# Expert columns of the last layer by one-hot products from resident rows, without a row table in DRAM

## The reference

```
s = sigmoid(t @ w_router)                       # 16 experts in 4 groups
eidx = the two best experts inside the best group
for e in range(16):
    y = (silu(t @ w_gate[e]) * (t @ w_up[e])) @ w_down[e]   # 1024 -> 512 -> 1024, float32
    out = out + combine[:, e:e+1] * y
```

## Time and profile before

| | |
|---|---|
| median of 3 runs | 1370.53 us (1370.07 to 1372.29) |
| profiled execution, its own time | 1371.52 us |
| its span, first to last instruction | 1369.4 us |
| busy: PE, PEld, DVE, ACT, POOL | 1243.1, 783.0, 622.9, 369.1, 124.5 us |
| moved by DMA | 382.73 MB, mean 279 GB/s |
| mean granted PE clock | 0.967 |

### The profile page before, as it was taken

How to read it: one execution, slowest core, us unless ns; L and a number is a source line. 1 busy time by engine, 2 the same in 40 slices (tenths; PEclk the granted TensorE clock), 3 DMA queues, 4 the chain that set the end, 5 groups by cost and what they waited for, 6 DMA issues and landing times.

```text
span 1369.4 us, 20046 instructions
## 1 busy us (share of the span) xinstructions
PE 1243.1 (91%) x8172; PEld 783.0 (57%) x8172; DVE 622.9 (45%) x1122; ACT 369.1 (27%) x599; POOL 124.5 (9%) x119
## 2 busy tenths in 40 slices
PE   4799999999999898999989957899999988998996
PEld 1577688787777633433333336787889833443443
DVE  2728467786464542211131127577876562221222
ACT  2523234442253310100100015544546420000000
POOL 0000000000022020000000020007930310000000
PEclk9999999999999999999999977999999999999998
DMA  9734469463635579999899982875354779999996
GB/s 380 292 134 198 167 246 383 132 223 123 246 123 219 215 277 343 339 355 354 307 373 401 414 315 110 334 314 213 124 154 154 309 290 367 399 387 398 398 420 250
DMA packets 59887, 382.73 MB, mean 279 GB/s; under 512 B 8912, under 2 KB 11412, under 8 KB 20308
## 3 DMA queue, kind: packets, MB, share of 16 engines
q1 hardware_dynamic: 45584, 345.00, 65.1%
q10 hardware_dynamic: 9748, 18.74, 4.2%
q0 software_dynamic: 4464, 17.71, 3.6%
HBM read 363.84 MB, written 44.84 MB: 298 GB/s over the span
## 4 chain that ended last, share of the span: by engine, by line
issue 22%; PE 19%; DMA 14%; DVE 6%; ACT 2%; POOL 2%; SPq 0%; DVEq 0%; POOLq 0%; ACTq 0%
DMA wexp<-in_expert 11%; PE bank L2045 3%; PE bank L2047 3%; PE bank L2046 3%; PE bank L2467 3%; DMA x_rows<-trow,rowid 2%; PE bank L2452 1%; PE bank L2013 1%; PE bank L2485 1%; POOL x_rows L782 1%; PE bank L2055 1%; POOL m_lo L766 1%; PE bank L2137 1%; DMA stage<-in_in 1%; PE bank L2325 1%
## 5 line engine op out<-in xcount | busy, mean ns | idle before, releaser
L2452 PE MATMUL bank<-wexp,xg 128*64 128x512 f32 (+1 forms) x1488 | 264.9, 598 | 12.4 <-DMA wexp<-in_expert 9.4
L2045 PE MATMUL bank<-h_hi,whi 128*128 128x512 f32 (+1 forms) x640 | 224.8, 351 | 15.9 <-DVE h_lo L1271 11.7
L2047 PE MATMUL bank<-h_hi,wlo 128*128 128x512 f32 (+1 forms) x640 | 219.6, 343 | 0.0
L2046 PE MATMUL bank<-h_lo,whi 128*128 128x512 f32 (+1 forms) x640 | 219.6, 343 | 0.0
L2452 PEld LDWEIGHTS bank<-wexp,xg 128*64 128x64 f32 (+1 forms) x1488 | 77.3, 125 | 164.3 <-issue 143.1
L2467 PE MATMUL bank<-wexp,act_a 128*32 128x256 f32 (+1 forms) x1072 | 150.6, 505 | 19.5 <-DMA wexp<-in_expert 15.3
L1271 DVE TENSOR_TENSOR wlo<-stage,whi 128x2048 fp32r<-128x2048 f32 x56 | 133.7, 2395 | 40.3 <-ACT whi L809 28.4
L2045 PEld LDWEIGHTS bank<-h_hi,whi 128*128 128x128 f32 x640 | 124.1, 194 | 40.0 <-issue 14.6
L1271 DVE TENSOR_TENSOR act_a<-act_s,bank 128x256 f32<-128x256 f32 (+1 forms) x47 | 17.2, 365 | 256.7 <-ACT act_s L809 256.7
L2046 PEld LDWEIGHTS bank<-h_lo,whi 128*128 128x128 f32 x640 | 123.9, 194 | 13.5 <-issue 0.5
L2047 PEld LDWEIGHTS bank<-h_hi,wlo 128*128 128x128 f32 x640 | 123.6, 193 | 13.7
(11 more groups left out here) (343 smaller groups left out, 1599.5 us busy)
## 6 DMA issues: line engine op xcount, KB each, us to landing
wexp<-in_expert SPq DMA_DIRECT2D x190, 1024.0 KB, 15.4
stage<-in_in SPq DMA_DIRECT2D x40, 1024.0 KB, 8.5
raw<-in_mod SPq DMA_DIRECT2D x18, 1024.0 KB, 7.0
stage<-in_mod SPq DMA_DIRECT2D x16, 1024.0 KB, 4.9
x_rows<-in_c_zero SPq DMA_DIRECT2D x32, 512.0 KB, 7.7
y_rows<-in_c_zero SPq DMA_DIRECT2D x20, 512.0 KB, 7.8
spare<-in_mod SPq DMA_DIRECT2D x8, 1024.0 KB, 16.9
stage<-in_out SPq DMA_DIRECT2D x8, 1024.0 KB, 4.8
```

The lines of the kernel that those rows point to most:

```text
L2045: MM(o, w[0], x_[0], start=start, stop=False)
L2046: MM(o, w[0], x_[1], start=False, stop=False)
L2047: return MM(o, w[1], x_[0], start=False, stop=stop)
L2452: ins = MM(bank[0][g * w:(g + 1) * w, :], x_[:, 2 * j + k, :], weights[:, c], start=(first_ == 0), stop=(last_ == 0))
```

## The change

In the last layer every step's columns, those of the extra items too, are made in one go by products: the stationary operand is a 128 x 128 tile of `trow`, the moving one is the step's one-hot matrix, 64 or 32 columns wide, and two products (one for each tile of tokens) add up in `bank[1]`, so that no transpose follows. That is 8 x 2 = 16 float32 products in a step. DVE makes the one-hot matrices in a ring of three (`pick_n`, `match_n`): steps 0 to 3 ahead of the loop as in the first layer, then that of step s + 4 at the end of step s, then one in each extra item, with the table row kept in `row_now`. The last layer has no `x_rows` table, no scatters, no loads to `xpick`, no `step_rows` and no `picked_out`; the 12 zeroing blocks of its table go too. `SIDE` is 4: pieces 0 to 3 of the first ranked expert have buffers of their own (the two new ones where `xpick` lay), and SP's wait for the scatters is gone. The first layer's steps are the same.

```diff
-PICKED = (4, 2)
+PICKED = 4
-SIDE = (0, 2)
+SIDE = (0, 4)
...
+        side = [at_byte(f"side{j}", [P, 2048], f32, off) for j, off in enumerate((R2 + 8 * K, GLU, R3, R3 + 8 * K))]
+        SIDE_SEMS = ("spare_a", "spare_b", "side_c", "side_d")
...
-        x_rows = [nc.dram_tensor(f"x_rows{l}", (ROWS[l], D), f32, kind="Internal").ap() for l in range(DEPTH)]
+        x_rows = nc.dram_tensor("x_rows", (ROWS, D), f32, kind="Internal").ap()
...
@@ SP @@
-                            for rows_ in (*x_rows, y_rows):
-                                if b * P < rows_.shape[0]:
-                                    load("all", "rows_zeroed", rows_[b * P:(b + 1) * P, :], A["c_zero"])
+                            for rows_ in (x_rows, y_rows):
+                                load("all", "rows_zeroed", rows_[b * P:(b + 1) * P, :], A["c_zero"])
...
-                    if l == DEPTH - 1 and (r, j) == (plan.aside, plan.side):
-
-                        sp.wait_ge(sem("all", "scattered"), sum(2 * (span(i) // P) for i in range(DEPTH)) * 16)
@@ POOL @@
-                for t in range(T // P):
+                for t in range(T // P if l == 0 else 0):
...
-                for i in range(XR - 1):
+                for i in range(XR - 1 if l == 0 else 0):
@@ ACT @@
-                for s in range(2):
+                for s in range(2 if l == 0 else 0):
                     picked_out(s)
...
-                    if s == PICKED[l] - 1:
+                    if l == 0 and s == PICKED - 1:
-                        act.wait_ge(sem("all", "scattered"), sum(2 * (span(i) // P) for i in range(l + 1)) * 16)
+                        act.wait_ge(sem("all", "scattered"), 2 * NT * 16)
...
-                    if PICKED[l] <= s <= STEPS - XR + 1:
+                    if l == 0 and PICKED <= s <= STEPS - XR + 1:
@@ DVE @@
+                def pick_step(s, first_row, w, slot):
+                    v.then(ts(adj[:, :, 0:NT], tokv[:, 4:6, 0:NT], first_row, None, SUB))
+                    m_ = match_[:, :, 0:NT * w].rearrange("p c (t w) -> p c t w", w=w)
                     at_ = iota[:, 0:w].unsqueeze(1).to_broadcast([P, NT, w])
                     for c in range(2):
                         v.step(tt(m_[:, c, :, :], at_, adj[:, c, 0:NT].unsqueeze(2).to_broadcast([P, NT, w]), ALU.is_equal))
                     v.sync()
...
+                    if l > 0 and (not isinstance(s, int) or s >= 3):
+                        dve.wait_ge(S("xT_mm"), s - 2)
+                    tt(pick_[:, slot, 0:NT * w], match_[:, 0, 0:NT * w], match_[:, 1, 0:NT * w], ADD).then_inc(S("picked"), 1)
                     dve.wait_ge(S("picked"), s + 1)
...
+                    if l == DEPTH - 1 and PICKED <= s + 4 < STEPS:
+                        pick_step(s + 4, float(plan.steps[s + 4][3]), plan.steps[s + 4][4], (s + 4) % 3)
...
                 with dve.Fori(0, count) as i:
+                    if l == DEPTH - 1:
+                        pick_step(i + STEPS, row_now[:, 1:2], E, STEPS % 3)
                     columns(i + STEPS, E)
@@ PE @@
+                def picked_columns(s, slot, w):
+                    pe.wait_ge(S("picked"), s + 1)
+                    for k in range(KT):
+                        for i in range(NT):
+                            t = row_tile(l, NT + i)[0]
+                            if isinstance(s, int) and s == 0 and k == 0:
+                                pe.wait_ge(S("h2"), NS * KT + i + 1)
+                            ins = MM(bank[1][:, k * w:(k + 1) * w], trow[:, t, k * P:(k + 1) * P], pick_n[:, slot, t * w:(t + 1) * w], start=(i == 0), stop=(i == NT - 1))
+                    ins.then_inc(S("xT_mm"), 1)
...
-                    w, r = plan.steps[s][4], s - PICKED[l]
-                    if r >= 0:
+                    w, r = plan.steps[s][4], s - PICKED
+                    if l == DEPTH - 1:
+                        picked_columns(s, s % 3, w)
+                    elif r >= 0:
...
-                for s in range(2):
+                for s in range(2 if l == 0 else 0):
                     step_rows(s)
...
-                    pe.wait_ge(S(f"xload{LAST % XR}"), row_loads(LAST) + i * 16)
-                    pe.sem_inc(sem("all", "passed"), 1)
-                    columns(LAST % XR, E)
+                    if l == 0:
+                        pe.wait_ge(S(f"xload{LAST % XR}"), row_loads(LAST) + i * 16)
+                        pe.sem_inc(sem("all", "passed"), 1)
+                        columns(LAST % XR, E)
+                    else:
+                        picked_columns(s, STEPS % 3, E)
```

More of the change, by code:

```diff
@@ L208, in hybrid_backbone @@
     E = HALF_STEP
-    ROWS = [-(-(p.extra_base + (p.extra + 1) * E) // P) * P for p in plans]
-    assert ROWS[0] == max(ROWS) and ROWS[0] // P == 20
+    ROWS = -(-(plans[0].extra_base + (plans[0].extra + 1) * E) // P) * P
+    assert ROWS // P == 20
     TWO_PI_HI, TWO_PI_LO, ROUND = 6.28125, 2 * math.pi - 6.28125, 1.5 * 2.0 ** 23
@@ L490, in hybrid_backbone @@
         row_now = at_byte("row_now", [P, 2], f32, R6 + 256)
+        pick_n = at_byte("pick_n", [P, 3, 2 * C], f32, R6 + 3 * K)
+        match_n = at_byte("match_n", [P, 2, 2 * C], f32, R6 + 4 * K + 512)
         yg = at_byte("yg", [P, 4, 2, D], f32, R1)
@@ L775, in _ @@
                 if l == 0:
-                    pool.wait_ge(sem("all", "rows_zeroed"), (sum(ROWS) // P + ROWS[0] // P) * 16)
-                pool.wait_ge(S("h2"), seqs(l) * KT + T // P)
-                pool.wait_ge(S("rowid_ok"), 1)
-                for t in range(T // P):
+                    pool.wait_ge(sem("all", "rows_zeroed"), 2 * (ROWS // P) * 16)
+                    pool.wait_ge(S("h2"), seqs(l) * KT + T // P)
+                    pool.wait_ge(S("rowid_ok"), 1)
+                for t in range(T // P if l == 0 else 0):
                     for c in range(2):
                         pool.indirect_dma_start(
-                            out=x_rows[l], out_offset=bass.IndirectOffsetOnAxis(ap=rowid[:, 2 * t + c:2 * t + c + 1], axis=0),
+                            out=x_rows, out_offset=bass.IndirectOffsetOnAxis(ap=rowid[:, 2 * t + c:2 * t + c + 1], axis=0),
                             in_=trow[:, t, :], in_offset=None,
                         ).then_inc(sem("all", "scattered"), 16)
-                pool.wait_ge(sem("all", "scattered"), sum(2 * (span(i) // P) for i in range(l + 1)) * 16)
-                for i in range(XR - 1):
-                    row, w = plans[l].steps[PICKED[l] + i][3:]
-                    load("all", f"yg{i}", xpick[0:w, i, :], x_rows[l][row:row + w, :])
+                if l == 0:
+                    pool.wait_ge(sem("all", "scattered"), 2 * (T // P) * 16)
+                for i in range(XR - 1 if l == 0 else 0):
+                    row, w = plans[l].steps[PICKED + i][3:]
+                    load("all", f"yg{i}", xpick[0:w, i, :], x_rows[row:row + w, :])
                 if l < DEPTH - 1:
@@ L1198, in _ @@
                         silu(s - 1, places[s - 1][1])
-                    if s + 2 < PICKED[l]:
+                    if l == 0 and s + 2 < PICKED:
                         picked_out(s + 2)
@@ L1767, in _ @@
                 dve.wait_ge(S("places"), 1)
+                pick_, match_ = (pick, match) if l == 0 else (pick_n, match_n)
                 if LEADERS[l]:
@@ L1773, in _ @@
                     for s in range(LEADERS[l]):
-                        v.step(tt(quick(match, s), iota[:, 0:C].unsqueeze(1).to_broadcast(shape), place[:, :, s].unsqueeze(2).to_broadcast(shape), ALU.is_equal))
+                        v.step(tt(quick(match_, s), iota[:, 0:C].unsqueeze(1).to_broadcast(shape), place[:, :, s].unsqueeze(2).to_broadcast(shape), ALU.is_equal))
                     v.sync()
@@ L1777, in _ @@
                         assert plans[l].steps[s][3:] == (plans[l].bases[s], C)
-                        tt(quick(pick, s), quick(match, s), e3(row(5))[:, :, s].unsqueeze(2).to_broadcast(shape), MUL).then_inc(S("picked"), 1)
+                        tt(quick(pick_, s), quick(match_, s), e3(row(5))[:, :, s].unsqueeze(2).to_broadcast(shape), MUL).then_inc(S("picked"), 1)
                 for i in range(1, NT):
@@ L1843, in _ @@
                     v.sync()
-                    if s >= 3:
+                    if l == 0 and s >= 3:
                         dve.wait_ge(S("rows"), 2 * NT + s - 2)
-                    tt(pick[:, s % 3, 0:NT * w], match[:, 0, 0:NT * w], match[:, 1, 0:NT * w], ADD).then_inc(S("picked"), 1)
+                    if l > 0 and (not isinstance(s, int) or s >= 3):
+                        dve.wait_ge(S("xT_mm"), s - 2)
+                    tt(pick_[:, slot, 0:NT * w], match_[:, 0, 0:NT * w], match_[:, 1, 0:NT * w], ADD).then_inc(S("picked"), 1)
                     dve.wait_ge(S("picked"), s + 1)
+                for s in range(LEADERS[l], PICKED):
+                    pick_step(s, float(plan.steps[s][3]), plan.steps[s][4], s % 3)
                 def items():
@@ L1949, in _ @@
```

(1 more changed line is left out.)

41 lines of the change are left out of this document (22 added, 19 removed).

## The result

The changed kernel takes 1409.4 us as the median of 4 runs (1399.25 to 1421.1), the kernel before 1370.3 us. The ratio of the two is 1.0263, with a 95% interval from 1.0227 to 1.03. Measured again (experiment 5) it took 1408.9 us (6 runs, 1405.0 to 1416.7), a ratio of 1.0295 (1.0258 to 1.0332). The profiled execution took 1411.58 us, its span 1409.8. Forecast were 1403 us and a range of 1384 to 1426. One of the four runs, 1421.1 us at a mean clock of 0.912, is left out of the ratio as disturbed; the median of the other three is 1407.3 us.

What follows compares the result with a forecast made beforehand. Weight stream ends last, PE close behind and taking over. Columns +60.6, waits -29.8, clock +8.5, start +1, extra pick +0.3, end -7.6 give +33.0, 1403 us; range 1384 to 1426 for 8 in 10.

Steps and rivals of the forecast that it cites:

- PE stood close behind, and takes over: Last layer's expert steps: the weight stream ends last, PE close behind; after the change PE bounds, no weight waits expected.
- the 29.8 us worked out: Last layer's expert steps: PE time lost to data waits and the half clock after some, all 29.8 us taken off.
- The price of a run: Each step's 32 column records: 4.16 us for 64 columns, 3.84 for 32; together +60.6 us of PE.
- rival B: Column records go at the replaced transposes' pace, 0.076 us each: -3.4 us, 1367 us; chance 0.06.
- Rival A: The clock falls in nearly every step of the last layer: +55 us, 1426 us; chance 0.16.
- Rival C: PE has room, weights stay the bound and the products hide: -17 us, 1353 us; chance 0.03.
- The clock: Last layer's steps: clock falls after narrow runs, 1.7 us each, 8.5 us in all; range 0 to 10 falls.
- The start: First columns before the last layer's expert steps, partly at half clock until about 1110.7 us: +1, bounds 0 and +4.
- the late start: Start of the last layer's steps: the clock rises later; counted as +3 in the high end of the range.
- The end: Extra item's gate and up 4.7 us less, `turn`, `combine` and `down` 2.9 less: together -7.6.
- Picks, side pieces, zeroing blocks at nothing: DVE's picks in the loop, two more side pieces and the removed zeroing blocks cost or gain nothing; extra item's pick +0.3.
- The table at nothing: Last layer's row loads, some 3.2 MB or 8.2 us, leave the stream: no gain beyond the waits already counted.

Runs made afterwards that it cites:

- experiment 5: The changed kernel measured again without any change: 1408.9 us, ratio 1.0295 to the kernel before.
- experiment 1: The changed kernel with two side pieces in place of four: 1412.2 us, ratio 1.0296 to the kernel before.
- experiment 8: Kernel with one-hot matrices stationary (1356.9 us), its weight stream held back after four side pieces until the first step's `act_a`: 1356.8 us.
- Experiment 2: The changed kernel with the run of records cut in two for steps 2 to 17, `down(s-1)` between the halves: 1401.3 us, ratio 1.0223.
- experiment 7: The changed kernel with only rows 0 to 63 of each token tile as stationary operand, 64 x 128: 1425.8 us, ratio 1.0402.
- experiment 3: The changed kernel with 64 columns moving in every record, in 32-row steps too: 1397.7 us, ratio 1.0196.
- experiment 10: The changed kernel with the 12 zeroing blocks put back in the first layer: 1413.2 us, ratio 1.0322.
- experiment 9: Kernel with one-hot matrices stationary (1356.9 us), plus the row table's scatters, SP's wait and unread row loads, two side pieces for four: 1366.7 us.

## Why the prediction was right

**PE stood close behind, and takes over.** Right. All 20.8 us of waits for weights (14.8 + 6.0, of which 3.4 in the end) are gone and nothing came back; PE rests only 2.0 us in the stretch, in the wait that was to stay. That the stretch lost the 29.8 us worked out is read from this and from the sum below, which closes. Experiments 1 and 8 show that the stream's start does not matter while PE has the longer path.

**The price of a run.** 4.16 us was taken for 64 columns and 3.84 for 32; the trace gives 3.72 and 3.69. Both lie at the lower row of the bounds, that of 2 columns moving, and not between: from 2 to 64 columns the width costs 0.1 us in 32 records. The row of `turn`, 0.13, was the nearest in form and misled, because it is so short. Experiment 2 shows it: 16 records take 1.90 us and 32 take 3.69, so 0.112 for each further record and 0.11 once for each run; 8 records would take 1.00 of `turn`'s 1.04 us. Dividing a run of 8 by 8 puts all of that 0.11 on its records. The term was 60.6 and measured 8 x 3.08 + 10 x 3.09 = 55.5 us at full clock. (The group has 608 records and not 576: those of step 0, which the prediction priced with the start, stand in it too.) The Trainium skill, "TensorE: Matmul & The Clock Gate", section "LDWEIGHTS (loading the stationary operand)", says that columns over 1.2 GHz set a load and rows do not. Experiment 7 agrees on the rows (3.69 us with 64 and with 128), and an estimate of 107 ns for 128 columns by that formula stands beside the 115 ns measured. That rule was named with rival B, but it speaks only of loads and not of transposes. That the load is what a record costs here is supported by PEld's 3.66 us in a run of 3.70, by the width that costs nothing and by the rows; it is not shown, since no run changed the number of stationary columns. A fixed price of 0.115 for any record is ruled out: `down` of a 32-row step has 32 records in 1.87 us. And it is not the price of every record with 128 stationary columns: `combine` of a 32-row step, whose products use four groups of 32 rows by turns, has 16 in 1.08 us, 0.068 each.

**Rival A** fell: six of 19 runs bring the clock down, not nearly all. **Rival B**, the pace of the transposes, fell with the price: 0.115 us a record against 0.076. Experiment 7 leaves the kind of the instruction as the difference, or the moving operand, an identity there; which of the two was not tried. **Rival C** fell with the first table of waits.

**The clock.** The mechanism was right and its size too small. Five falls of 1.7 us were taken, 8.5 us. The steps' stretch is 14.6 us longer than the sum of its pieces at full clock (229.87 - 29.8 + 52.5 for the 17 runs in it is 252.6). Read from start to start, five narrow runs and the work behind them account for 11.5 of that (1.6, 3.2, 3.3, 1.7 and 1.6 us), the first gate and up, partly at half clock (8.90 us in place of 7.02, 1117.87 to 1126.77), for 1.9, and a fall behind the 2.0 us wait for `spread`, in `combine` and `down`, for 1.6; together 15.0. The sixth narrow run costs 2.9 in the end, 0.7 in the run and 2.2 in gate and up. That makes 17.5 in place of 8.5. Narrow runs have 14.4 of it: the count, six against five, was nearly right, but three falls lasted twice as long as the one in the rows. The rest was in the sum at nothing. That narrow runs are to blame is shown from both sides by experiments 2 and 3, which take 8 and 12 us off. The falls are not at the same steps in each execution: the one profiled in experiment 10 has them behind the same six runs, that of experiment 1 behind these and a seventh, that of experiment 5 partly behind others. Whether this is why the changed kernel's runs lie 11.7 us apart in experiment 5 stays open; in experiment 1, with the same columns, they lie 4.8 apart, as close as those of experiments 2 and 3 (5.6 and 5.4).

**The start** was +1.6 against +1, close by luck. The clock was to be back at full by 1110.7 us, with 18 of the 30 records at 0.13; all 30 went at half clock, 0.22 each, and it rose only at about 1121.3, after 11 us of these records and gate and up. The 30 took 6.7 us where 5.2 were worked out, and the margin in the +1 took up more than half of the difference. The 1.9 of the first gate and up, counted with the clock above, was in the bound only (the late start). **The end** was to be 7.3 us shorter but for its run. It is 24.7 us where it was 26.05; less its columns at full clock, 3.7 and 0.6, and less the 2.9 of the clock, that is 18.1 against 25.4, 7.3 shorter. Right.

**Picks, side pieces, zeroing blocks at nothing.** Right, by the waits and experiments 1 and 10. **The table at nothing** was right for this change, where the stretch is 37 us longer and the DMA share 0.81, but not as a general reading: experiment 9.

Together, against the forecast of +33.0 for the profiled execution: 55.5 for columns, 29.8 back from the stretch, 17.5 for the clock in place of 8.5, 1.6 at the start, 7.3 back at the end with its pick, and 2.8 that came from before the steps, is 40.3, against 40.4 of the span and 40.1 measured. The median came out nearer to the forecast of 1403.5 us than the terms did: columns taken 5.1 too dear hid more than half of a clock term 9.0 too small.

## What to carry to other kernels

When two resources stand within a tenth of each other, add up the full demand of the second before work is moved to it: here 30 us of 230 were free and 55 were moved. The price of a long run of short records is better taken from two runs of different length than from one short run divided by its records. For picking a few columns by a one-hot product, make the narrow one-hot matrix stationary and let the wide rows move, even if transposes follow; with the wide rows stationary each record cost 0.115 us, whatever the number of columns. The long runs of records with 32 columns moving were worth breaking up or widening, 8 and 12 us here, since the rest of the step pays for them in clock; but in experiment 7, with half the rows, the clock fell after runs of 64 columns too.

## What the runs showed of the hardware that was not expected

With a 128 column stationary operand in float32 a record in a run of 32 took 0.1125 us with 2 columns moving, 0.115 with 32 and 0.116 with 64, and the same with 64 and 128 rows stationary. After runs of 32 such records the granted clock fell with 32 columns and 128 rows, not with 64 columns and 128 rows (238 us at 1.00), but again with 64 columns and 64 rows (0.89 over 255 us), though PE was busy throughout in all three. At the start, 30 records with 64 columns and 128 rows, 6.66 us without a gap, did not bring a clock at half back to full; in the kernel before, after 4 us of records that move 512 columns (1106.51 to 1110.50 at 0.50), it stood at 0.96 from 1110.50 to 1112.70. Three of the six falls lasted 6.8 us, twice the one in the kernel before; what sets that, and at which of the narrow runs the clock falls, stays open: in experiment 5 it was partly at others.
